# Decoder layer on one core: x loaded before the weights, split in two halves of its tokens, tile 0's low-weight products last

## The chip, the cores and the metric

One Trainium2 chip, one of its cores. The metric is the device time of one execution in microseconds (us); the kernel before takes 1079.82 us (median of 3 runs, 1078.2 to 1080.12). The engines are TensorE (PE, and PEld for its weight loads), VectorE (DVE), ScalarE (ACT), GpSimd (POOL) and SyncE (SP, which here issues nearly all DMAs).

## The reference

One layer of a decoder, 512 tokens, 1024 channels, all float32: RMSNorm, one input projection to three token mixers (RWKV-7, sparse attention, sliding-window attention) and to gates, merge, output projection, residual; then RMSNorm and a SwiGLU feed-forward with residual. What the change touches is only the first step:

```
y = x * rsqrt(mean(x*x) + eps) * g_pre_mix      # (512, 1024)
p = y @ w_in                                    # first columns: rwkv 0, 1, 2, ...
```

The kernel computes `(x * g_pre_mix)` transposed, multiplies it by the weights, and applies the row factor `rsqrt(...)` (`RINV`) when a result leaves PSUM.

## The kernel before

**Number format.** Products are as exact as float32 by splitting both sides in a high part (rounded to the engine's fp32r) and a low part (the rest). Each product of a chunk is three matmuls: high weight x high x (L1546), high weight x low x (L1547), low weight x high x (L1548). A weight tile `n` (1024 x 128) is loaded by SP to `WRAW` (four slots), its high part is written to `WHI` by ScalarE (L723; for tiles in `POOL_HI` by GpSimd, L609), its low part to `WLO` by GpSimd (L605). Semaphores `w_loaded`, `w_hi`, `w_lo` count them, in order of tiles. There are two slots of `WHI`/`WLO`, so the high part of tile n waits until tile n-2 is done.

**Tiles.** The jobs of `JOBS` run in order: tile 0 has 8 chunks `k` of 128 channels, each 3 matmuls of 128x128 weights by 512 tokens; its sum stands in PSUM bank 0, tile 1's in bank 1. `steps(c)` issues c chunks of the next tiles.

**The start.** SP issues x in four token tiles `x_in[t]` of 128 tokens x 1024 channels, the fourth after W0; then W1, `HOT`, `SNK`, `MASK`, W2, `SELT`, `WA`, W3; from W4 on each load waits for the low part of four tiles earlier. ScalarE issues the constants `CONP` (with the identity that transposes need) and the two parts of the parameter table `PRAW` on its own queue. TensorE transposes seven of eight channel blocks of x tiles 0, 1 and 2, then the table (its result goes to PSUM bank 7, and VectorE copies it to `PARC` in two pieces, `prow_ok`), then tile 3, then the eighth block of all four tiles, whose bank 7 the table had used. Bank k holds channel block k for all 512 tokens. ScalarE writes the high part of a block with its gain, `HHI[:, k]` (L739); VectorE writes the low part `HLO[:, k]` (L1106); chunk k of tile 0 waits for that (`xlo_ok`). Between them ScalarE squares and sums x tiles 0 and 2 and makes W0's high part; VectorE squares tiles 1 and 3 (L1096). From the sums come the root (L742), the reciprocal, four diagonal blocks (L1113, `diag_ok`) and, after four chunks of tile 1, one product (L1616) that spreads the factor over all partitions (`RINV`).

**The same pattern later.** The feed-forward's input is split in two halves of 256 tokens: `x1_transposes`, `h2_high` (L949) and `h2_low` (L1480), with the weights' products from L1961 on.

Of the kernel before, what the change touches and what calls it, by code (L numbers as in the profile page):

```python
# [24 lines left out]
F32 = mybir.dt.float32  # L25
# [8 lines left out]
KC = D // P  # L34
# [104 lines left out]
POOL_HI = [1] + list(range(NS0 + 4, MERGE0))  # L139
# [106 lines left out]
def build(nc, x, w_in, w_branch, w_out, w_gate, w_up, w_down, w2, a2, g2, ck1, ck2, cv1, cv2, sinks, rel_bias,  # L246
# [158 lines left out]

    def x1_block(h, k):
        return psum[(2, 3, 0, 1, 2, 3, 4, 6)[4 * h + k // 2]][:, 256 * (k % 2):256 * (k % 2) + 256]
# [124 lines left out]
    with block:  # L532
        @block.sync
        def _(sp):
# [3 lines left out]
            for t in range(3):  # L538
                x_tile(t)
            for n in range(FF0):  # L540
                if n == 1:
                    x_tile(3)
# [165 lines left out]
        def _(act):  # L708
# [7 lines left out]
            def hi_part(n):  # L716
# [4 lines left out]
                if n in (2, MERGE0):  # L721
                    act.wait_ge(w_hi, n)
# [9 lines left out]
            x_square(0)  # L732
            act.wait_ge(xsq_ok, 1)
            x_square(2)
            hi_part(0)
            act.wait_ge(prow_ok, 2)
            for k in range(KC):
                act.wait_ge(xT_done, k + 1)
                act.activation(HHI[:, k, :], psum[k][:, :], ACT.Identity, scale=par("g_pre_mix", k)).then_inc(xhigh_ok, 1)  # L739
# [282 lines left out]
        def _(dve):  # L1022
# [76 lines left out]
            x_square(1)  # L1099
            dve.wait_ge(prow_T, 1)  # L1100
            dve.tensor_copy(PARC[:, 0:NPAR1], R[5][:, 0:NPAR1]).then_inc(prow_ok, 1)
            dve.tensor_copy(PARC[:, NPAR1:NPAR1 + NPAR2], R[5][:, P:P + NPAR2]).then_inc(prow_ok, 1)
            dve.wait_ge(prow_ok, 2)
            for k in range(KC):
                dve.wait_ge(xhigh_ok, k + 1)
                dve.scalar_tensor_tensor(out=HLO[:, k, :], in0=psum[k][:, :], scalar=par("g_pre_mix", k),  # L1106
                                         in1=HHI[:, k, :].bitcast(F32), op0=ALU.mult, op1=ALU.subtract).then_inc(xlo_ok, 1)
# [422 lines left out]
        def _(pe):  # L1530
# [28 lines left out]
            def steps(count):  # L1559

                for _ in range(count):
# [11 lines left out]
                    if n == 0:  # L1573
                        pe.wait_ge(xlo_ok, k + 1)
# [6 lines left out]
                    if k == chunks - 1:  # L1581
                        last.then_inc(dense_done, 1)
                        dense["n"], dense["k"] = n + 1, 0

# [11 lines left out]
            def x_transpose(t, k):  # L1596
                return tr(psum[k][:, t * P:(t + 1) * P], XTOK0[:, t, k * P:(k + 1) * P])

            for t in range(3):
                pe.wait_ge(x_in[t], 16)  # L1600
                for k in range(KC - 1):
                    x_transpose(t, k)
# [3 lines left out]
            pe.wait_ge(x_in[3], 16)  # L1606
            for k in range(KC - 1):
                x_transpose(3, k).then_inc(xT_done, 1)
            pe.wait_ge(prow_ok, 2)
            for t in range(4):  # L1610
                last = x_transpose(t, KC - 1)
# [435 lines left out]
```

## Time and profile before

| | before |
|---|---|
| median of runs | 1079.82 us (1078.2 to 1080.12) |
| the profiled execution | 1081.36 us, span 1079.6 us |
| PE busy | 1045.2 us, 97% of the span |
| chain that ended last | PE 83%, DVE 9%, POOL 4% |
| mean granted clock of TensorE | 0.995 |

The profiled execution is one run, with its own time; its span is the stretch from the first to the last recorded instruction. In a timeline row the first number is the start from the span's start, the second the length; "x8" are eight instructions merged in one row; a bracket gives the idle time before and what ended it. A chain row tells which piece of work the end of the kernel hung on at that moment. Matmuls overlap: one takes 0.39 us from issue to end, while the next starts 0.23 us after it.

### The profile page before, as it was taken

To read this page: it belongs to the slowest core of one execution; us is meant where nothing else is said; L and a number is where in the kernel's file an instruction comes from. 1 tells how busy PE (TensorE), PEld (TensorE's weight loads), DVE (VectorE), ACT (ScalarE), POOL (GpSimd) and SP (SyncE) were. 2 spreads that over 40 slices of the span, in tenths; PEclk is the share of its full clock that TensorE was granted. 3 is DMA by queue.
4 is the path that set the end of the run, shared out by engine and by line. 5 is a ranking of instruction groups with operands and counts; after the bars stand their busy time and mean duration, and the time that the engine had idled before them with its cause. 6 is when DMAs were issued, how large, how long until landed. Compare 5 with 4: busy or idle time off the path is not lost.

```text
span 1079.6 us, 18610 instructions
## 1 busy us (share of the span) xinstructions
PE 1045.2 (97%) x7560; PEld 836.0 (77%) x7560; DVE 527.5 (49%) x882; ACT 355.8 (33%) x688; POOL 496.8 (46%) x409
## 2 busy tenths in 40 slices
PE   7989999999999999999989999999999999999997
PEld 6777778887787677766777777888888888888886
DVE  4775687466555545554552664144454545430004
ACT  4133332221322225444550445352222222221221
POOL 3365453113121446655777447534444444444462
PEclk9999999999999999999999999999999999999999
DMA  9334533002223453212112545603333333333322
GB/s 253 95 98 138 115 88 80 3 4 59 61 61 100 120 142 118 59 32 79 40 39 79 175 118 167 213 27 91 97 97 97 97 97 97 116 98 98 98 79 78
DMA packets 148784, 102.67 MB, mean 95 GB/s; under 512 B 20917, under 2 KB 131775, under 8 KB 148712
## 3 DMA queue, kind: packets, MB, share of 16 engines
q1 hardware_dynamic: 145516, 97.67, 31.9%
q10 hardware_dynamic: 3164, 3.97, 1.5%
q8 instruction: 53, 0.87, 0.4%
q14 instruction: 19, 0.16, 0.0%
q0 software_dynamic: 32, 0.00, 0.0%
HBM read 93.99 MB, written 7.63 MB: 94 GB/s over the span
## 4 chain that ended last, share of the span: by engine, by line
PE 83%; DVE 9%; POOL 4%; issue 2%; ACT 1%; DMA 1%; SPq 0%; ACTq 0%; DVEq 0%; POOLq 0%
PE ps L1546 17%; PE ps L1548 15%; PE ps L1547 15%; PE ps L1685 4%; PE ps L2001 4%; PE ps L2000 4%; PE ps L1999 4%; PE ps L1592 4%; PE ps L1845 3%; PE ps L1897 2%; DVE XF L1074 1%; PE ps L1921 1%; PE ps L1922 1%; PE ps L1923 1%; POOL WLO L605 1%
## 5 line engine op out<-in xcount | busy, mean ns | idle before, releaser
L605 POOL TENSOR_TENSOR WLO<-WRAW,WHI 128x1024 fp32r<-128x1024 f32 (+1 forms) x131 | 293.9, 2244 | 283.6 <-ACT WHI L723 158.0
L1546 PE MATMUL ps<-HHI,WHI 128*128 128x512 f32 x776 | 316.9, 408 | 5.1 <-POOL WLO L640 2.3
L1548 PE MATMUL ps<-HHI,WLO 128*128 128x512 f32 x776 | 304.3, 392 | 0.0
L1547 PE MATMUL ps<-HLO,WHI 128*128 128x512 f32 x776 | 304.1, 392 | 0.0
L1546 PEld LDWEIGHTS ps<-HHI,WHI 128*128 128x128 f32 x776 | 146.6, 189 | 57.7 <-issue 22.0
L1548 PEld LDWEIGHTS ps<-HHI,WLO 128*128 128x128 f32 x776 | 146.5, 189 | 32.0
L1547 PEld LDWEIGHTS ps<-HLO,WHI 128*128 128x128 f32 x776 | 146.8, 189 | 29.3 <-issue 1.9
L609 POOL CAST WHI<-WRAW 128x256 fp32r<-128x256 f32 (+1 forms) x78 | 49.2, 631 | 179.8 <-PE ps L1548 179.8
L723 ACT ACTIVATE WHI<-WRAW 128x1024 fp32r<-128x1024 f32 (+1 forms) x69 | 62.5, 907 | 159.4 <-PE ps L1548 82.0
L1504 DVE TENSOR_TENSOR FT<-FT 128x512 f32<-128x512 f32 x22 | 51.6, 2348 | 89.0 <-ACT FT L977 89.0
L870 ACT ACTIVATE EB<-EB,STAT 128x257 f32<-128x257 f32 (+5 forms) x96 | 50.4, 527 | 55.7 <-DVE STAT L1388 54.6
L971 ACT ACTIVATE WHI<-WRAW 128x1024 fp32r<-128x1024 f32 x40 | 42.3, 1057 | 71.7 <-PE ps L1548 71.7
L2001 PE MATMUL ps<-WLO,DHI 128*128 128x512 f32 x160 | 62.3, 389 | 0.0
L1999 PE MATMUL ps<-WHI,DHI 128*128 128x512 f32 x160 | 62.3, 389 | 0.0
L2000 PE MATMUL ps<-WHI,DLO 128*128 128x512 f32 x160 | 62.3, 389 | 0.0
L667 POOL TENSOR_SCALAR EB<-EB,STAT,GLT 128x128 f32<-128x128 f32 (+3 forms) x64 | 38.1, 608 | 33.2 <-DVE STAT L1404 33.0
L640 POOL TENSOR_TENSOR WLO<-WRAW,WHI 128x256 fp32r<-128x256 f32 x56 | 43.0, 768 | 4.6
L979 ACT ACTIVATE DHI<-FT 128x512 f32 (+1 forms) x22 | 13.9, 632 | 88.6 <-DVE FT L1509 88.6
L1388 DVE CUSTOM_DVE_ANT_0 EB<-ps,TB 128x128 f32<-128x128 f32 (+3 forms) x64 | 28.2, 488 | 25.3 <-PE ps L1845 25.3
L1546 PE MATMUL ps<-OHI,WHI 128*128 128x512 f32 x96 | 38.2, 398 | 2.0 <-POOL WLO L605 2.0
L1547 PE MATMUL ps<-OLO,WHI 128*128 128x512 f32 x96 | 37.4, 390 | 0.0
L1548 PE MATMUL ps<-OHI,WLO 128*128 128x512 f32 x96 | 37.4, 389 | 0.0
(311 smaller groups left out, 1608.1 us busy)
## 6 DMA issues: line engine op xcount, KB each, us to landing
WRAW<-in_w_in SPq DMA_DIRECT2D x47, 512.0 KB, 4.3
WRAW<-in_w_gate SPq DMA_DIRECT2D x22, 512.0 KB, 3.9
WRAW<-in_w_up SPq DMA_DIRECT2D x22, 512.0 KB, 3.9
WRAW<-in_w_down SPq DMA_DIRECT2D x22, 512.0 KB, 3.9
spilled<-SQ SPq DMA_DIRECT2D x21, 256.0 KB, 2.5
WRAW<-in_w_in SPq DMA_DIRECT2D x16, 256.0 KB, 3.6
WRAW<-in_w_branch SPq DMA_DIRECT2D x32, 128.0 KB, 2.9
WRAW<-in_w_out SPq DMA_DIRECT2D x8, 512.0 KB, 4.0
```

Source lines behind the costliest of these rows:

```text
L605: return pool.tensor_tensor(lo[:, 0:chunks, :], WRAW[:, n % NRAW, 0:chunks, :], hi[:, 0:chunks, :].bitcast(F32), ALU.subtract)
L609: return pool.tensor_copy(WHI[:, slot_of(n), k0:k1, :], WRAW[:, n % NRAW, k0:k1, :])
L723: act.activation(split_of(n)[0][:, 0:width_of(n), :], WRAW[:, n % NRAW, 0:width_of(n), :], ACT.Copy).then_inc(w_hi, 1)
L870: last = act.activation(EB[:, n % 3, g, cols], EB[:, n % 3, g, cols], ACT.Exp, scale=-1.0, bias=st[:, 0, u:u + 1], accum_out=st[:, 1, u:u ...
L1504: dve.tensor_tensor(FT[:, b + 1, :], FT[:, b + 1, :], FT[:, b, :], ALU.mult).then_inc(ff_x, 1)
L1546: pe.matmul(dst, WHI[:, s, k, :], hi, start=start, stop=False)
L1547: pe.matmul(dst, WHI[:, s, k, :], lo, start=False, stop=False)
L1548: return pe.matmul(dst, WLO[:, s, k, :], hi, start=False, stop=stop)
L1592: return pe.transpose(dst, src, ident[0:n, 0:n])
L1999: pe.matmul(dst, DHI[:, k, cols], whi, start=start, stop=False)
L2000: pe.matmul(dst, DLO[:, k, cols], whi, start=False, stop=False)
L2001: return pe.matmul(dst, DHI[:, k, cols], wlo, start=False, stop=stop)
```

## The change

- SP issues all four x tiles before W0.
- Banks 0 to 3 now hold all eight channel blocks of tokens 0 to 255, banks 4 to 7 those of tokens 256 to 511 (`x_block`). TensorE's order is x tile 0, the table, x tile 1, a wait for the copies to `PARC`, x tiles 2 and 3. `xT_done` counts pairs of blocks.
- ScalarE writes 16 high parts of 256 tokens instead of 8 of 512, behind the square of tile 0 and a wait for the copies; then comes the high part of W1 (it had W0's), then the square of tile 2. GpSimd makes W0's high part (it had W1's).
- VectorE copies the table before it squares tile 1 and writes 16 low parts of 256 tokens, each waiting for its pair of high parts (they share a bank).
- Tile 0's eight chunks issue their two products with the high weights first (wait `w_hi`), each after the low part of the second half; the eight products with the low weights come last, behind a wait for W0's low part.

```diff
--- before.py
+++ after.py
@@ -136,7 +136,7 @@
 NJ = len(JOBS)
 NRAW, NSPL = 4, 2
 
-POOL_HI = [1] + list(range(NS0 + 4, MERGE0))
+POOL_HI = [0] + list(range(NS0 + 4, MERGE0))
 
 SPILLED = list(range(SW0, GC0))
 NSTAGE = 2
@@ -402,6 +402,9 @@
 
     def down_bank(t, dh):
         return psum[4 + t if dh == 0 else t]
+
+    def x_block(h, k):
+        return psum[4 * h + k // 2][:, 256 * (k % 2):256 * (k % 2) + 256]
 
     def x1_block(h, k):
         return psum[(2, 3, 0, 1, 2, 3, 4, 6)[4 * h + k // 2]][:, 256 * (k % 2):256 * (k % 2) + 256]
@@ -535,11 +538,9 @@
             def x_tile(t):
                 sp.dma_start(XTOK0[:, t, :], x[t * P:(t + 1) * P, :]).then_inc(x_in[t], 16)
 
-            for t in range(3):
+            for t in range(4):
                 x_tile(t)
             for n in range(FF0):
-                if n == 1:
-                    x_tile(3)
                 if n == 2:
                     sp.dma_start(HOT[:, :], hot).then_inc(hot_in, 16)
                     sp.dma_start(SNK, bass.AP(sinks.tensor, 0, [[0, P], [1, NH]])).then_inc(hot_in, 16)
@@ -718,7 +719,7 @@
                 act.wait_ge(w_loaded[n % NRAW], loaded_value(n))
                 if slot_free(n):
                     act.wait_ge(dense_done, slot_free(n))
-                if n in (2, MERGE0):
+                if n in (1, MERGE0):
                     act.wait_ge(w_hi, n)
                 act.activation(split_of(n)[0][:, 0:width_of(n), :], WRAW[:, n % NRAW, 0:width_of(n), :],
                                ACT.Copy).then_inc(w_hi, 1)
@@ -730,13 +731,15 @@
                                accum_out=XSS[:, t:t + 1]).then_inc(xsq_ok, 1)
 
             x_square(0)
+            act.wait_ge(prow_ok, 2)
+            for h in range(2):
+                for k in range(KC):
+                    act.wait_ge(xT_done, 4 * h + k // 2 + 1)
+                    act.activation(HHI[:, k, 256 * h:256 * h + 256], x_block(h, k), ACT.Identity,
+                                   scale=par("g_pre_mix", k)).then_inc(xhigh_ok, 1)
+            hi_part(1)
             act.wait_ge(xsq_ok, 1)
             x_square(2)
-            hi_part(0)
-            act.wait_ge(prow_ok, 2)
-            for k in range(KC):
-                act.wait_ge(xT_done, k + 1)
-                act.activation(HHI[:, k, :], psum[k][:, :], ACT.Identity, scale=par("g_pre_mix", k)).then_inc(xhigh_ok, 1)
             act.wait_ge(xsq_ok, 2)
             act.wait_ge(xsum_ok, 2)
             act.activation(XRINV, XSS, ACT.Sqrt, scale=1.0 / D, bias=EPSC[:, 0:1]).then_inc(norm_std, 1)
@@ -1096,15 +1099,17 @@
                 dve.tensor_tensor_reduce(TMP[:, 0:2, :].rearrange("p a t -> p (a t)"), XTOK0[:, t, :], XTOK0[:, t, :],
                                          1.0, 0.0, ALU.mult, ALU.add, XSS[:, t:t + 1]).then_inc(xsum_ok, 1)
 
-            x_square(1)
             dve.wait_ge(prow_T, 1)
             dve.tensor_copy(PARC[:, 0:NPAR1], R[5][:, 0:NPAR1]).then_inc(prow_ok, 1)
             dve.tensor_copy(PARC[:, NPAR1:NPAR1 + NPAR2], R[5][:, P:P + NPAR2]).then_inc(prow_ok, 1)
+            x_square(1)
             dve.wait_ge(prow_ok, 2)
-            for k in range(KC):
-                dve.wait_ge(xhigh_ok, k + 1)
-                dve.scalar_tensor_tensor(out=HLO[:, k, :], in0=psum[k][:, :], scalar=par("g_pre_mix", k),
-                                         in1=HHI[:, k, :].bitcast(F32), op0=ALU.mult, op1=ALU.subtract).then_inc(xlo_ok, 1)
+            for h in range(2):
+                for k in range(KC):
+                    cols = slice(256 * h, 256 * h + 256)
+                    dve.wait_ge(xhigh_ok, 8 * h + 2 * (k // 2) + 2)
+                    dve.scalar_tensor_tensor(out=HLO[:, k, cols], in0=x_block(h, k), scalar=par("g_pre_mix", k),
+                                             in1=HHI[:, k, cols].bitcast(F32), op0=ALU.mult, op1=ALU.subtract).then_inc(xlo_ok, 1)
             dve.wait_ge(xsum_ok, 1)
             x_square(3)
             dve.wait_ge(norm_std, 1)
@@ -1570,8 +1575,6 @@
                             pe.wait_ge(xsplit_ok, i + 1)
                         if kind == "branch":
                             pe.wait_ge(olo_ok, 4 * (i % 3) + 4)
-                    if n == 0:
-                        pe.wait_ge(xlo_ok, k + 1)
                     hi, lo = rhs(n, k)
                     if kind == "cmp":
                         last = cmp_product(n, k, hi, lo, part == 0 and k == 0, part == 3 and k == 3)
@@ -1582,6 +1585,19 @@
                         last.then_inc(dense_done, 1)
                         dense["n"], dense["k"] = n + 1, 0
 
+            def first_tile():
+
+                pe.wait_ge(w_hi, 1)
+                for k in range(KC):
+                    pe.wait_ge(xlo_ok, KC + k + 1)
+                    pe.matmul(DB[0][:, :], WHI[:, 0, k, :], HHI[:, k, :], start=k == 0, stop=False)
+                    pe.matmul(DB[0][:, :], WHI[:, 0, k, :], HLO[:, k, :], start=False, stop=False)
+                pe.wait_ge(w_lo, 1)
+                for k in range(KC):
+                    last = pe.matmul(DB[0][:, :], WLO[:, 0, k, :], HHI[:, k, :], start=False, stop=k == KC - 1)
+                last.then_inc(dense_done, 1)
+                dense["n"] = 1
+
             def fill(point):
                 steps(FILL[point])
 
@@ -1593,24 +1609,23 @@
 
 
             pe.wait_ge(con_in, 16)
-            def x_transpose(t, k):
-                return tr(psum[k][:, t * P:(t + 1) * P], XTOK0[:, t, k * P:(k + 1) * P])
-
-            for t in range(3):
+            def x_transposes(t):
                 pe.wait_ge(x_in[t], 16)
-                for k in range(KC - 1):
-                    x_transpose(t, k)
+                for k in range(KC):
+                    at0 = P * (t % 2)
+                    last = tr(x_block(t // 2, k)[:, at0:at0 + P], XTOK0[:, t, k * P:(k + 1) * P])
+                    if t % 2 and k % 2:
+                        last.then_inc(xT_done, 1)
+
+            x_transposes(0)
             pe.wait_ge(par_in, 32)
             tr(R[5][:, 0:NPAR1], PRAW[0:NPAR1, 0, :], NPAR1)
             tr(R[5][:, P:P + NPAR2], PRAW[0:NPAR2, 1, :], NPAR2).then_inc(prow_T, 1)
-            pe.wait_ge(x_in[3], 16)
-            for k in range(KC - 1):
-                x_transpose(3, k).then_inc(xT_done, 1)
+            x_transposes(1)
             pe.wait_ge(prow_ok, 2)
-            for t in range(4):
-                last = x_transpose(t, KC - 1)
-            last.then_inc(xT_done, 1)
-            steps(8)
+            x_transposes(2)
+            x_transposes(3)
+            first_tile()
             steps(4)
             pe.wait_ge(diag_ok, 4)
             pe.matmul(R[4][:, :], ones, SSUM[:, :], start=True, stop=True).then_inc(norm_ss, 1)
```

## Rows read from the trace of the kernel before

**Rows 1.** Page, parts 1 and 4: busy time (share of the span), chain by engine

```profile
PE 1045.2 (97%) x7560; PEld 836.0 (77%) x7560; DVE 527.5 (49%) x882; ACT 355.8 (33%) x688; POOL 496.8 (46%) x409
...
PE 83%; DVE 9%; POOL 4%; issue 2%; ACT 1%; DMA 1%; SPq 0%; ACTq 0%; DVEq 0%; POOLq 0%
```

**Rows 2.** Chain of waits, 5 to 22 us: start, length, what

```profile
2.94 9.35 DMA XTOK<-in_x
...
12.34 2.61 PE ps L1592 x11
14.94 0.43 PE ps L1546
...
17.34 0.23 PE ps L1546
...
21.46 0.23 PE ps L1546
```

**Rows 3.** Timeline, 0 to 12 us, all engines

```profile
2.14 0.76 SPq L570 DMA_DIRECT2D WRAW<-in_w_in  x1
...
2.94 1.66 SPq L536 DMA_DIRECT2D XTOK<-in_x  x1
...
5.28 1.75 PE L1592 MATMUL ps<-CONP,XTOK 128*128 128x128 f32 x7 [5.28 <-DMA CONP<-in_con]
...
9.41 1.06 ACT L729 ACTIVATE SQ<-XTOK 128x1024 f32<-128x1024 f32 x1 [3.26 <-DMA XTOK<-in_x]
...
10.92 0.62 PE L1592 MATMUL ps<-CONP,PRAW 74*128 74x74 f32 x2
10.99 1.06 ACT L723 ACTIVATE WHI<-WRAW 128x1024 fp32r<-128x1024 f32 x1 [0.42 <-DMA WRAW<-in_w_in]
...
11.74 0.21 DVE L1102 COPY PARC<-ps 128x64 f32<-128x64 f32 x1
```

**Rows 4.** DMA issued at 2 to 3 us (landing), packets at 7:8, 8.5:8.8

```profile
WRAW<-in_w_in SPq DMA_DIRECT2D x1, 512.0 KB, 8.8
...
q10 hardware_dynamic: 24, 0.01, 3.7%
...
q10 hardware_dynamic: 4, 0.00, 1.5%
```

**Rows 5.** Timeline, 12 to 28 us, all engines

```profile
12.13 2.36 POOL L605 TENSOR_TENSOR WLO<-WRAW,WHI 128x1024 fp32r<-128x1024 f32 x1 [10.14 <-ACT WHI L723]
...
12.91 4.74 ACT L739 ACTIVATE HHI<-ps,PARC 128x512 fp32r<-128x512 f32 x8 [0.86 <-PE ps L1592]
...
13.70 5.36 DVE L1106 SCALAR_TENSOR_TENSOR HLO<-ps,PARC,HHI 128x512 fp32r<-128x512 f32 x8 [1.75 <-ACT HHI L739]
...
14.44 1.03 POOL L609 CAST WHI<-WRAW 128x1024 fp32r<-128x1024 f32 x1
...
18.98 1.22 DVE L1096 CUSTOM_DVE_ANT_0 TMP<-XTOK 128x1024 f32<-128x1024 f32 x1
...
20.85 0.88 DVE L1113 TENSOR_SCALAR SSUM<-CONP,MISC 128x128 f32<-128x128 f32 x4
...
24.02 1.02 PE L1616 MATMUL ps<-SSUM,CONP 128*128 128x512 f32 x2
```

**Rows 6.** Timeline, 700 to 727 us, feed-forward input, second half: ACT, DVE, PE

```profile
716.33 3.02 ACT L949 ACTIVATE HHI<-ps,PARC 128x256 fp32r<-128x256 f32 x8 [5.80 <-PE ps L1592]
...
717.20 3.23 DVE L1480 SCALAR_TENSOR_TENSOR HLO<-ps,PARC,HHI 128x256 fp32r<-128x256 f32 x8 [6.07 <-ACT HHI L949]
...
717.74 0.39 PE L1961 MATMUL ps<-HHI,XWHI 128*128 128x256 f32 x1 [1.45 <-DVE HLO L1480]
```

**Rows 7.** Timelines of POOL and DVE, 0 to 90 us

```profile
36.53 2.40 POOL L605 TENSOR_TENSOR WLO<-WRAW,WHI 128x1024 fp32r<-128x1024 f32 x1 [5.11 <-ACT WHI L723]
...
36.78 2.69 DVE L1130 SCALAR_TENSOR_TENSOR RW<-PSH,PARC,RW 128x512 f32<-128x512 f32 x1
...
75.83 0.75 DVE L1130 SCALAR_TENSOR_TENSOR RW<-PSH,PARC,RW 128x512 f32<-128x512 f32 x1
```

## Prediction

> **What bounds the kernel now.** I read the page's busy times and chain first. TensorE is busy 97% of the span and holds 83% of the chain that ended last [rows 1]; almost everything between about 17 us and the end is a queue of 512-column products at 0.23 us each. A change in the first 20 us is therefore worth exactly what it moves the moment at which that queue starts, and nothing more, as long as nothing behind it becomes late.
>
> The chain of waits for the first 22 us says what sets that moment [rows 2]: the fourth token tile of x is issued at 2.94 and lands 9.35 us later, at 12.29; eleven transposes follow until 14.94; then tile 0's 24 products. The first five of them stand 0.43 us apart and the later ones 0.23. These are the two levels of the engine's clock, 1.2 and 2.4 GHz (the ratio is 1.87), although the granted clock prints as full; the engine had been busy without a break since 12.34 when the spacing fell at 17.1 to 17.3. Tile 1's first product starts at 21.46. The reference point of the whole sum is this 21.46: "tile 0 done".
>
> Then the timeline of each engine, to see who could have started earlier [rows 3]. The seven transposes of a token tile take 1.75 us (0.22 us each, low clock). The transposes of the parameter table start at 10.92, and VectorE's two copies, which everything that scales by `g_pre_mix` waits for, end at 11.95. Before, the table's transposes stand behind three x tiles, so one cannot see when the table really landed, only that it was by 10.9.
>
> **What replaces the wait.** The wait for x tile 3 goes. SP issues it in the slot in which W0 was issued (2.14 instead of 2.94 [rows 3]), and the transfers land roughly in order of issue: x tile 2 by 9.4, W0 at 10.98 (2.14 + 8.8 [rows 4]), x tile 3 at 12.29. Swapped, x tile 3 lands at about 11.0 and W0 at about 12.3. What is late next is the parameter table. In the new order its transposes stand in front of those of x tile 1, so that its landing holds TensorE, both copies on VectorE, and through them ScalarE's first high part. The table comes on ScalarE's own queue, q10. That queue still moves 24 packets between 7 and 8 us and 4 between 8.5 and 8.8 [rows 4]. So the table lands after 8.8 and before 10.92. I take 9.5, since x tile 2, whose packets shared the engines with it until then, lands at 9.37. TensorE thus goes idle after x tile 0, from about 7.1 to 9.5: the earlier x tile buys nothing until then.
>
> The Trainium skill, "DMA: Bandwidth & Descriptors", section "Why a DMA increments its semaphore by 16 and not by 1", says that a transfer is dealt over the largest number of engines up to 16 that divides its rows, which makes two for 74 rows. It would explain why 37 KB trickle for so long; the packet counts show the trickle, no row shows the two engines.
>
> **The sum, from T = 9.7, the first product of the table's transposes** (9.5 plus the 0.2 us of a weight load). Offsets are those of before: copies done at T + 1.03 (11.95 - 10.92) = 10.73; TensorE free at T + 0.62 = 10.3.
>
> - x tile 1: 8 transposes x 0.22 = 1.8, until 12.1; tile 2 until 13.8, tile 3 until 15.6 at the low clock. Tile 3 has landed long before.
> - ScalarE, half 0: its first high part came 0.57 us after the transpose that it needed (12.34 to 12.91 [rows 2, 5]); now it needs the pair, so 10.52 + 0.57 = 11.1. A 128x256 high part is not in the first 20 us, but the same form stands at the FFN's input: 8 in 3.02 us [rows 6], 0.365 apart. Half 0 runs 11.1 to 14.1.
> - VectorE: square of x tile 1 now stands behind the copies: 10.75 + 1.22 [rows 5] = 12.0. Then 8 low parts of half 0 at 3.23 us per eight [rows 6], 0.394 apart: 12.05 to 15.2. High parts are ahead of them.
> - ScalarE, half 1: first pair of tile 3 starts at 14.0, + 0.57 = 14.6 (14.3 if the clock is up by then); high parts until 17.4. VectorE half 1 starts when both are ready, 15.2 to 15.45.
> - TensorE's first product of tile 0: in the FFN's pair of rows the first product comes 0.54 us after the first low part starts (717.20 to 717.74 [rows 6]): 15.85. Later low parts come every 0.394 us and two products take 0.454, so TensorE is never held again; the last low part is due at 18.6, its product at 19.0.
> - 24 products x 0.227 = 5.45, taken at the high level, since TensorE then has been at work from 9.5, with a pause of 0.2 at most (before, it had worked from 12.34 when the spacing fell at 17.3): tile 0 done at 21.3, against 21.46. Gain 0.16, call it 0.2 us.
>
> The first product starts 0.9 us later than before (15.85 against 14.94), and the 1.07 us that the slow products cost there (21.46 - 14.94 = 6.52, less 5.45) comes back. Bounds: the landing anywhere from 8.8 to 10.7 shifts everything by -0.7 to +1.2.
>
> **Costs that I put at nothing, and their cover.** W0's high part on GpSimd: W0 at 12.3 plus one cast of 1.03 [rows 5] is 13.4, cover 2.4 us before 15.85. Its low part (2.36 [rows 5]) ends at 15.8; it is needed after 16 products, at 19.5. The products of the low weights placed last cost the same 8 x 0.227, wherever they stand. W1's high part on ScalarE now stands behind 16 high parts: 1.06 [rows 3], 17.4 to 18.5, its low part until 20.9; TensorE wants it at 21.3: cover 0.4 us, the thinnest. Norm of x: square of tile 3 starts at 18.5 and the chain from there to the last diagonal took 2.75 us before (18.98 to 21.73 [rows 5]), so 21.3; needed after 12 products of tile 1, at 24.0. ScalarE's x square of tile 2 (1.06 [rows 3]) falls in the gap between W1's high part and the root. W2's high part waits behind the root, 0.3 to 0.8 later than before, and tile 2 is wanted only after 24 more products. SP waits for W0's low part before it issues W4, 1.3 us later (15.8 against 14.5), and for W1's before W5 (20.9 against some 17.8); four earlier loads still fill the queue, and tile 4 is wanted not before 21.46 + 3 x 5.45 = 37.8.
>
> One cover is at risk. A VectorE operation with two SBUF inputs does not run beside a GpSimd one: the `L1130` operation takes 0.75 alone but 2.69 when it starts inside a low part of 36.53 to 38.93, and ends 0.5 after it [rows 7]. The new square of tile 3 starts at 18.5, just as W1's low part does. If GpSimd is first, the square ends at about 21.9 and the diagonals at 23.4, still before 24.0. If VectorE is first, W1's low part ends up to 1.2 later, at 22.1, and TensorE stands 0.8 us. The Trainium skill, "GPSIMD Engine Reference", section "Specifications", says the same: the SBUF interfaces are shared, with contention for VectorE instructions with two SBUF inputs. The low parts of half 0 and 1 read one input from PSUM, and before they ran beside two GpSimd operations at 0.67 us each.
>
> **Own time.** The profiled execution took 1081.36 us with a span of 1079.6; the median of the runs is 1079.82, 1.5 lower, with runs from 1078.2 to 1080.12. The gain of 0.2 is applied to the median: 1079.6 us.
>
> **Rivals.**
>
> A, the forecast: the table's landing takes the place of x tile 3's. 1079.6. Chance 0.59.
>
> B, the table is there by 7.1, q10's late packets being something else. TensorE never idles, T = 7.3, tile 0 done 2.4 earlier in all clocked alike, less a few slow products: 1077.6. For it: nothing shows the landing itself. Against: the packets until 8.8, and q10 carries only the table after the constants. Chance 0.13.
>
> C, the clock rises at the same point as before, 17.1, not earlier: three or four of tile 0's products at 0.43, +0.6 to 0.8 on A: 1080.3. Against: the unbroken work begins 2.6 us sooner. Chance 0.10.
>
> D, the port: VectorE's square gets in front of W1's low part, TensorE stands 0.8 us at tile 1: 1080.4. Chance 0.07.
>
> E, slower: x tile 3's 4 KB packets now stand where W0's 512 B ones stood, and q10's packets share the DMA engines with them. If the table is pushed back until x tile 3 is through, it lands at 12.3, where x tile 3 landed before; T = 12.5, tile 0 done at 24.1, + 2.7: 1082.5. It decides from a landing of 11.8 on. For it: the table was slow beside 4 KB packets before. Against: its last packets go out by 8.8, while x tile 2 is still on its way, so few turns are left to lose. Chance 0.11. The Trainium skill, "DMA: Bandwidth & Descriptors", section "Queues, rings and completion order", says that a DMA engine takes turns between queues packet by packet, which is the mechanism of E; by that rule each turn lost costs one 4 KB packet.
>
> **How the numbers follow.** No change can be told from one of less than 0.2%, 2.2 us. A, C and D lie inside; B is at that edge (0.10 of its 0.13 beyond it, as a table landing before 7 would bring nothing more and the runs scatter by 1 us), and A's low tail adds 0.05: faster 0.15. E gives 0.08 beyond, the upper tails of A, C and D 0.04: slower 0.12. Same 0.73. Range for 8 in 10: from B's time, 1077.6, to the landing at its late bound on top of A with the scatter of the runs, 1081.6. The likeliest case's own range is 1078.7 to 1080.8.
>
> **What would show it.** TensorE idle from about 7 to 9.5 us with the release by the table's DMA; the copies to `PARC` ending near 10.7; ScalarE's half 0 from 11.1 and VectorE's half 1 from 15.3; first product of tile 0 near 15.9 at the high clock; tile 1's first product near 21.3, no wait on `WLO`; the norm's product near 24.0. The prediction is wrong if TensorE does not idle before the table (B), if it idles beyond 11 (E), if the low parts do not follow each other at 0.39, or if a stage after 25 us does not simply move along with tile 0.

## The result, and the profile after

The changed kernel takes 1081.53 us (median of 16, 1079.87 to 1083.32) against 1079.95 (16, 1078.07 to 1080.76) for the kernel before on the same chip: a ratio of 1.0018, interval 1.001 to 1.0026. A second comparison gave 1081.75 against 1080.22, 1.0026 (1.0017 to 1.0035). It is slower by about 1.6 us. The prediction was 1079.6, 0.2 us faster; the measured time lies just inside its range for 8 in 10 (1077.6 to 1081.6) and above the range of its likeliest case (1078.7 to 1080.8).

The page of the changed kernel, its busy times, beside [rows 1]. The profiled execution took 1080.04 us with a span of 1078.2, and so looks shorter than the one of before; why is told at the end.

```profile
PE 1042.4 (97%) x7560; PEld 834.4 (77%) x7560; DVE 530.6 (49%) x890; ACT 356.1 (33%) x696; POOL 497.6 (46%) x409
```

The counts fit the edit: eight operations more on VectorE and on ScalarE, none on TensorE. The chain of waits of the same trace, 0 to 22 us (start, length, what), beside [rows 2]:

```profile
1.79 7.24 DMA PRAW<-in_par
...
9.07 4.73 PE ps L1608 x20
...
16.85 0.96 ACT WHI L724
...
17.87 3.43 POOL WLO L606
21.35 0.50 PE ps L1551
```

Where the chain of before began with x tile 3, this one begins with the parameter table. It ends in something that the chain of before did not have: tile 1 waits for the low part of W1, which takes 3.43 us instead of 2.4. The timeline of the same trace (a bracket is the idle time before, and its releaser):

```profile
9.07 0.68 PE L1608 MATMUL ps<-CONP,PRAW 74*128 74x74 f32 x2 [1.80 <-DMA PRAW<-in_par]
...
15.32 0.47 PE L1593 MATMUL ps<-HHI,WHI 128*128 128x512 f32 x1 [0.36 <-DVE HLO L1111]
...
21.35 0.50 PE L1551 MATMUL ps<-HHI,WHI 128*128 128x512 f32 x1 [0.34 <-POOL WLO L606]
```

In this execution T, the first product of the table's transposes, is 9.07, and tile 1 starts at 21.35, as before, where the timeline has tile 0's and tile 1's first products at

```profile
14.60 0.77 PE L1546 MATMUL ps<-HHI,WHI 128*128 128x512 f32 x1
...
21.30 0.39 PE L1546 MATMUL ps<-HHI,WHI 128*128 128x512 f32 x1
```

Such a start explains no 1.6 us. So the first question was whether this trace is typical.

### The profile page after: what moved, and what is told of

Same layout as the page of the kernel before. It is cut to its first block, busy times and chain, and to the rows that moved or that the text cites. A ratio compares the mean times of both kernels' runs of the same rounds, so it can differ in the third digit from the quotient of the medians.

```text
span 1078.2 us, 18628 instructions
## 1 busy us (share of the span) xinstructions
PE 1042.4 (97%) x7560; PEld 834.4 (77%) x7560; DVE 530.6 (49%) x890; ACT 356.1 (33%) x696; POOL 497.6 (46%) x409
## 4 chain that ended last, share of the span: by engine, by line
PE 82%; DVE 9%; POOL 4%; issue 2%; ACT 2%; DMA 1%; ACTq 0%; DVEq 0%; POOLq 0%
PE ps L1551 16%; PE ps L1553 15%; PE ps L1552 15%; PE ps L1700 4%; PE ps L1608 4%; PE ps L2016 4%; PE ps L2014 4%; PE ps L2015 4%; PE ps L1860 3%; PE ps L1912 2%; POOL WLO L606 1%; DVE XF L1077 1%; PE ps L1936 1%; PE ps L1938 1%; PE ps L1937 1%
## 5 line engine op out<-in xcount | busy, mean ns | idle before, releaser
L1551 PE MATMUL ps<-HHI,WHI 128*128 128x512 f32 x768 | 312.3, 407 | 5.4 <-POOL WLO L641 2.3
L1553 PE MATMUL ps<-HHI,WLO 128*128 128x512 f32 x768 | 300.0, 391 | 0.0
L1552 PE MATMUL ps<-HLO,WHI 128*128 128x512 f32 x768 | 299.5, 390 | 0.0
L1551 PEld LDWEIGHTS ps<-HHI,WHI 128*128 128x128 f32 x768 | 144.2, 188 | 57.9 <-issue 22.1
L1553 PEld LDWEIGHTS ps<-HHI,WLO 128*128 128x128 f32 x768 | 144.2, 188 | 31.3
L1552 PEld LDWEIGHTS ps<-HLO,WHI 128*128 128x128 f32 x768 | 144.5, 188 | 28.6 <-issue 1.9
```

The source lines that it names most:

```text
L1551: pe.matmul(dst, WHI[:, s, k, :], hi, start=start, stop=False)
L1552: pe.matmul(dst, WHI[:, s, k, :], lo, start=False, stop=False)
L1553: return pe.matmul(dst, WLO[:, s, k, :], hi, start=False, stop=stop)
```

## The experiments

The theories: **D**, VectorE's square stretches W1's low part (the expectations call it the stall theory); **C**, the clock; **S**, something after 25 us does not move along with tile 0; and **L**, formed only after the second trace, the table lands later than in the first trace in most executions, because x tile 3's packets stand beside it (the prediction's E in part). "Tile 1" below is the start of its first product: in the two traces of before 21.30 and 21.64, mean 21.47.

**The changed kernel again, timed and traced** (no edit).

> The changed kernel once more, as it is, to have a second trace and the spread on this chip. Clock theory: the two kernels do the same work in the same time at the same clock (the traces at hand are 0.2 us apart at 47 us and 0.3 at the end once one low-clock stretch of before is taken out), and the 1.6 us of the medians come from TensorE being at its low clock more often or longer; then times come in groups about 1.7 us apart and tile 0 ends at 20.6 in some traces and up to 1.7 later in others. Stall theory: the whole difference is the 0.76 us that TensorE stands before tile 1 and what it sets off; then tile 0 ends at 20.6 and tile 1 starts at 21.3 in each trace, and the time is 1080 to 1082.

Measured: 1081.75 us (11 runs) against 1080.22, 1.0026 (1.0017 to 1.0035). Timeline:

```profile
10.39 0.68 PE L1608 MATMUL ps<-CONP,PRAW 74*128 74x74 f32 x2 [3.11 <-DMA PRAW<-in_par]
...
12.73 6.50 DVE L1111 SCALAR_TENSOR_TENSOR HLO<-ps,PARC,HHI 128x256 fp32r<-128x256 f32 x16
...
16.64 0.47 PE L1593 MATMUL ps<-HHI,WHI 128*128 128x512 f32 x1 [0.79 <-DVE HLO L1111]
...
19.15 1.21 DVE L1099 CUSTOM_DVE_ANT_0 TMP<-XTOK 128x1024 f32<-128x1024 f32 x1
19.19 3.43 POOL L606 TENSOR_TENSOR WLO<-WRAW,WHI 128x1024 fp32r<-128x1024 f32 x1 [3.16 <-ACT WHI L724]
...
22.67 0.50 PE L1551 MATMUL ps<-HHI,WHI 128*128 128x512 f32 x1 [0.31 <-POOL WLO L606]
```

T is 10.39, TensorE idles 3.11 us for the table, and everything stands 1.32 us later than in the first trace, offset by offset: first product at T + 6.25 in both, tile 1 at T + 12.28 in both. Neither of the two theories of the expectation has a late table. What came true of it is that the times fall into groups (1081.6 to 1081.8 and 1082.7 to 1083.5). Of the traces that follow, all with this order of loads have T at 10.4 or later and the first one is the exception. How rare it is among executions is not shown: in the first comparison seven of 16 runs lie at 1079.9 to 1080.7, near its own 1080.04, in this one none of 11.

**Each kernel once more**, a third trace of the change and a second of before.

> The changed kernel, for one more trace. If the table lands late as a rule: its transposes at 10.3 to 10.8. If the first trace (9.07) is the rule: 9.0 to 9.3.

> The kernel before, for a second trace. x tile 3 lands at 12.2 to 12.6, tile 1 starts at 21.2 to 21.6, and q10's last packets go out by 9.0; a landing of x tile 3 that varies by over 0.5 us would say that the start of before is no firmer than that of the change.

First the change (1083.14 us), then before (1079.95):

```profile
10.46 0.68 PE L1608 MATMUL ps<-CONP,PRAW 74*128 74x74 f32 x2 [3.27 <-DMA PRAW<-in_par]
...
22.74 0.50 PE L1551 MATMUL ps<-HHI,WHI 128*128 128x512 f32 x1 [0.31 <-POOL WLO L606]
```

```profile
12.25 1.42 PE L1592 MATMUL ps<-CONP,XTOK 128*128 128x128 f32 x11 [1.00 <-DMA XTOK<-in_x]
...
21.64 0.39 PE L1546 MATMUL ps<-HHI,WHI 128*128 128x512 f32 x1
```

Mean of the change's two later traces 22.70, of before 21.47: + 1.23 of the 1.6 us, all of it ahead of 23 us. Tile 0's first products are not always fast before the change either: in the second trace of before eight of them come 0.4 us apart, five in the first, which is why tile 1 starts 0.34 later there.

**The change with x tile 3 behind W0 again**: only SP's order is undone.

```
-            for t in range(4):
+            for t in range(3):
                 x_tile(t)
             for n in range(FF0):
+                if n == 1:
+                    x_tile(3)
```

> The changed kernel with x tile 3 issued behind W0 again, as in the kernel before. Turn theory (the table's packets on q10 take turns with what SP's queue has at the front of each DMA engine, and behind 4 KB rows of x tile 3 a turn is dearer than behind 512 B runs of W0): q10's last packets go out by 9.0 instead of 9.5 to 10.3, the table's transposes start at 9.2 to 9.8 instead of 10.4 to 10.7, x tile 3 lands at 12.3, just in time for its transposes; median 0.7 to 1.2 us below the changed kernel's. Rival (the table is late whatever stands in SP's queue): start at 10.4 to 10.7 in the trace, same median as the changed kernel, 1081.7.

Measured: 1081.34 us (11) against 1080.20, 1.0014 (1.0005 to 1.0023).

```profile
9.62 0.68 PE L1610 MATMUL ps<-CONP,PRAW 74*128 74x74 f32 x2 [2.19 <-DMA PRAW<-in_par]
...
21.89 0.50 PE L1553 MATMUL ps<-HHI,WHI 128*128 128x512 f32 x1 [0.34 <-POOL WLO L608]
```

The trace is as the turn theory expected: T is 0.8 us earlier, and so is tile 1. The median is not: it is 0.2 to 0.4 us below the changed kernel's two medians instead of 0.7 to 1.2.

**Before with x tile 3 ahead of W0**, the same edit alone, the other way:

```
-            for t in range(3):
+            for t in range(4):
                 x_tile(t)
             for n in range(FF0):
-                if n == 1:
-                    x_tile(3)
```

> The kernel before with one edit, x tile 3 issued ahead of W0. If the late table is what the early x tile costs: x tile 3 lands at 10.1 to 10.6, but the table's transposes, which stand before those of tile 3, now start at 10.4 to 10.9 and let them follow at 11.5; tile 1's first product 0.5 to 0.8 us earlier than the 21.3 of before, median 1079.4 to 1079.9. If the early x tile alone made the kernel slower: above 1081.

Measured: 1081.45 us (11) against 1080.20, 1.0014 (1.0003 to 1.0024); an execution of 3606.67 us is left out.

```profile
10.84 0.49 PE L1590 MATMUL ps<-CONP,PRAW 74*128 74x74 f32 x2 [0.21 <-DMA PRAW<-in_par]
11.26 1.42 PE L1590 MATMUL ps<-CONP,XTOK 128*128 128x128 f32 x11
...
15.96 0.50 PE L1544 MATMUL ps<-HHI,WHI 128*128 128x512 f32 x1 [3.28 <-POOL WLO L603]
...
23.14 0.39 PE L1544 MATMUL ps<-HHI,WHI 128*128 128x512 f32 x1
```

L stands. With x tile 3 ahead of W0, T was 10.39, 10.46, 10.56, 10.70, 10.70 and 10.84 in six traces of five kernels (the first trace's 9.07 is the seventh); with W0 ahead 9.62, with nothing else changed. The last packet of q10, ScalarE's queue, tells the same and can be seen where the table's landing is hidden too: it starts at 8.6, 8.7 and 8.9 in the three traces with W0 ahead (two of before, and the change with W0 ahead), at 9.7 to 10.1 in the six with x tile 3 ahead, and at 8.5 in the first trace, whose cause stays open.

The swap alone makes the old kernel slower too, against what its expectation put first (0.5 to 0.8 us gained at tile 1, a median of 1079.4 to 1079.9). It is another wait that does it: x tile 3's transposes start 1.1 us sooner (11.26 against 12.34 [rows 2]), but TensorE then stands 3.28 us for W0's low part, eight of tile 0's products come 0.4 us apart, and tile 1 starts at 23.14. That wait is the one that placing the low products last hides: in the change W0's low part ends at 16.0 and is wanted at 20.4.

The packets say how the swap delays the table. DMA of a stretch by queue (packets, MB, share of 16 engines), 8.0 to 8.5 us: before, then the change again.

```profile
q1 hardware_dynamic: 259, 0.15, 110.4%
q10 hardware_dynamic: 8, 0.00, 2.7%
```

```profile
q1 hardware_dynamic: 54, 0.19, 96.1%
q10 hardware_dynamic: 7, 0.00, 2.4%
```

And the change again from 9.0 to 9.5 us, where before, its repetition and the kernel with W0 ahead have no q10 packet left:

```profile
q1 hardware_dynamic: 287, 0.16, 112.2%
q10 hardware_dynamic: 6, 0.00, 2.0%
```

SP's queue moves 259 packets in half a microsecond when they are W0's 512 B, and 54 when they are x's 4 KB. An estimate from the shares in these rows (16 engines, 0.5 us): one took 0.03 us when small, 0.14 when large. Against the small ones q10 gets its last packets out by 9.0, against the large ones 8 are left (6 here, 2 until 10.0). The Trainium skill, "DMA: Bandwidth & Descriptors", section "Queues, rings and completion order", says that an engine alternates between queues packet by packet; the runs agree with it in kind, since q10 is slower beside the larger packets. How many of the profile's packets go in one turn no row shows.

The landing of x tile 3 itself, issued at 2.14 in the change again (the last number is the time from issue to landing):

```profile
XTOK<-in_x SPq DMA_DIRECT2D x1, 512.0 KB, 8.5
```

So x tile 3 lands at 10.6, 0.2 us behind T: in this order the table does come in with the end of x tile 3. In the first trace x tile 3 takes 7.9 us, until 10.1, and the table is there 1.0 us before it.

**The table's first part as 64 + 10 rows**, in the change and in before (the same edit in `consts`, with the wait on 48):

```
-            act.dma_start(PRAW[0:NPAR1, 0, :], par1).then_inc(par_in, 16)
+            act.dma_start(PRAW[0:64, 0, :], par1[0:64, :]).then_inc(par_in, 16)
+            act.dma_start(PRAW[64:NPAR1, 0, :], par1[64:NPAR1, :]).then_inc(par_in, 16)
```

> The changed kernel with the first part of the parameter table loaded in two DMAs, of 64 and of 10 rows, instead of one of 74. Theory of the forecast (the table's landing sets the start): it lands by 7 us instead of 9.0, the copies end by 8.3, half 0 starts at 8.6, and tile 0's first product at 13.5 to 13.9, 1.5 to 1.8 us earlier; the time falls by as much. Rival (the rows are not what makes it late, the queue is): it lands at 9 as before and nothing changes.

> The kernel before with the table's first part in DMAs of 64 and of 10 rows. There the table's landing is hidden behind three x tiles. If the 74 rows also hold back what shares their DMA engines, x tile 3 lands at 11.3 to 11.5 instead of 12.3 and the time falls by 0.8 us; if they cost only themselves, nothing changes, median within 0.3 us of the kernel before.

Measured: the change 1079.38 us (11) against 1080.22, 0.9999 (0.999 to 1.0007); before 1078.54 (12) against 1080.20, 0.9991 (0.9983 to 1.0). Timelines, the change first:

```profile
8.51 0.68 PE L1609 MATMUL ps<-CONP,PRAW 74*128 74x74 f32 x2 [1.25 <-DMA PRAW<-in_par]
...
20.79 0.50 PE L1552 MATMUL ps<-HHI,WHI 128*128 128x512 f32 x1 [0.30 <-POOL WLO L606]
```

```profile
11.26 2.37 PE L1593 MATMUL ps<-CONP,XTOK 128*128 128x128 f32 x11 [1.68 <-DMA XTOK<-in_x]
...
19.72 0.39 PE L1547 MATMUL ps<-HHI,WHI 128*128 128x512 f32 x1
```

T comes 1.9 us earlier in the change (8.5, where 7 was expected), tile 1 as well, and the median falls by 2.4. So the table's landing is what the changed kernel waits for. But the same edit helps the kernel before too, by 1.7 us, twice the 0.8 that its expectation named for this case: x tile 3 lands at 11.2 instead of 12.3. The 74-row load had slowed the x tiles as well. The Trainium skill, "DMA: Bandwidth & Descriptors", section "Why a DMA increments its semaphore by 16 and not by 1", has a rule by which 74 rows go to two engines; both kernels agree with it, in that 64 + 10 rows move faster and clear the way for others, though no row shows which engines carried them. With the split in both, the change stays behind: tile 1 at 20.79 against 19.72, and 0.8 us in the medians, about half of the original loss; the two ratios' intervals overlap, so the 0.8 rests on the traces more than on the times.

**The table's first part on SP's queue, ahead of x**, in the change, without and with the square of x tile 3 on ScalarE:

```
+            sp.dma_start(PRAW[0:64, 0, :], par1[0:64, :]).then_inc(par_in, 16)
+            sp.dma_start(PRAW[64:NPAR1, 0, :], par1[64:NPAR1, :]).then_inc(par_in, 16)
             for t in range(4):
```

> The changed kernel with the table's first part in front of x on SP's queue, in DMAs of 64 and of 10 rows, and nothing else: c1_sp_table with the square of x tile 3 back on VectorE. Theory: copies at 8.5, tile 0's first product at 13.7 as there; W1's low part meets the square again and takes 3.4 us, 15.9 to 19.3, so that tile 1 starts 0.3 us later at most; what ScalarE's square seemed to cost at 290 us (0.3) does not occur; the median is within 0.5 us of c1_sp_table's. Rival (the port collision matters): 0.7 to 1.5 us slower than c1_sp_table.

> The changed kernel with the table's first part in front of x on SP's queue, in DMAs of 64 and of 10 rows, and the square of x tile 3 on ScalarE. Theory: table there before x tile 0 is transposed, its transposes at 7.3 to 7.6, tile 0's first product at 13.5 to 14.0 against 15.3 to 16.6, no stop before tile 1, tile 1's first product at 19.2 to 19.8; 1.5 to 2 us below the kernel before, 1078.2 to 1078.8. Rival (an early start meets W0, the clock or the weights instead): tile 1's first product at 20.5 or later and 1079.4 or more.

Measured: 1079.78 us (11), 0.9995 (0.9986 to 1.0003), T 7.79, tile 1 19.41; with the square on ScalarE 1079.20 (12, two of them at 1612 and 1717 us; 1078.5 without these), 0.9991 (0.998 to 1.0001), T 7.62, tile 1 19.24. This is rival B made real: T at about 7.7 gives a start 2.1 us ahead of before's, and medians lower by only 0.4 and 1.7. The lead is not lost in the trace of the first: it took 1077.99 us, 2.0 less than the second trace of before. What differs between its runs (four at 1077.9 to 1078.5, seven at 1079.6 to 1080.5) is taken up under "From 1.2 to 1.6 us". Its expectation failed on both counts: W1's low part was not stretched, since GpSimd started ahead of VectorE, and the median is over 0.5 us above the second kernel's (1.3 without that one's two long executions), on another chip. The rows of the first:

```profile
16.10 2.41 POOL L608 TENSOR_TENSOR WLO<-WRAW,WHI 128x1024 fp32r<-128x1024 f32 x1 [0.29 <-ACT WHI L725]
...
16.36 3.22 DVE L1100 CUSTOM_DVE_ANT_0 TMP<-XTOK 128x1024 f32<-128x1024 f32 x1
...
19.41 0.39 PE L1552 MATMUL ps<-HHI,WHI 128*128 128x512 f32 x1
```

Here the square pays (3.22 instead of 1.21 us) and TensorE does not stand. The expectation for the second held: tile 1 at 19.24 without a stop before it (19.2 to 19.8 expected), and 1078.5 without the two long executions (1078.2 to 1078.8).

**The square of x tile 3 on ScalarE alone**:

```
             act.wait_ge(xsq_ok, 2)
-            act.wait_ge(xsum_ok, 2)
+            x_square(3)
+            act.wait_ge(xsq_ok, 3)
+            act.wait_ge(xsum_ok, 1)
...
-            dve.wait_ge(xsum_ok, 1)
-            x_square(3)
```

> The changed kernel with the square of x tile 3 on ScalarE (behind that of tile 2) instead of VectorE, so that nothing of VectorE's with two SBUF inputs meets W1's low part on GpSimd. Stall theory: the low part takes 2.4 us instead of 3.4, is done at 20.3, TensorE goes from tile 0 to tile 1 without a stop at 20.6, and the time falls by 0.7 to 1.6 us. Clock theory: by 0.7 at most in executions with an early clock, by nothing in those with a late one; the spread stays.

Measured: 1082.65 us (8), 1.0025 (1.0015 to 1.0036).

```profile
19.50 2.40 POOL L606 TENSOR_TENSOR WLO<-WRAW,WHI 128x1024 fp32r<-128x1024 f32 x1 [3.16 <-ACT WHI L724]
...
22.48 0.39 PE L1551 MATMUL ps<-HHI,WHI 128*128 128x512 f32 x1
```

T is 10.70 here. W1's low part is back at 2.40, and tile 1 starts at T + 11.78 without a wait, 0.50 sooner than T + 12.28. So D is shown as a mechanism and sized, 0.5 us, at this place. In the medians it does not show (1082.65 against 1081.75, intervals overlapping), though 0.7 to 1.6 us less was expected. A part is given back: near 290 us TensorE waits 1.0 us for VectorE's `ST` in this trace and in the other one with the square on ScalarE, 0.7 in all others. Its eight runs lie at 1081.5 to 1081.8 and 1082.6 to 1083.5, as those of the change do.

**Ten transposes of nothing after x tile 0**, so that TensorE works while it waits for the table:

```
             x_transposes(0)
+            for _ in range(10):
+                tr(psum[7][:, 256:384], ident)
```

> The changed kernel with ten further transposes of the identity (2.2 us at 0.22) behind those of x tile 0, into a part of bank 7 that is written again later, so that TensorE does not idle from 7 to 9 us. Clock theory: the clock rises earlier and in every execution before tile 0, the upper groups of times go, median 1.0 to 1.7 us below the changed kernel's. Stall theory: no change within 0.5 us.

Measured: 1081.93 us (12), 1.0018 (1.0009 to 1.0027). Timeline, then the windows (length, busy time and count of each engine, granted clock, DMA share, GB/s):

```profile
10.98 2.84 PE L1608 MATMUL ps<-CONP,XTOK 128*128 128x128 f32 x24
...
16.34 0.47 PE L1593 MATMUL ps<-HHI,WHI 128*128 128x512 f32 x1 [2.52 <-DVE HLO L1111]
...
23.50 0.39 PE L1551 MATMUL ps<-HHI,WHI 128*128 128x512 f32 x1
```

```profile
16.70:20.10 3.40, 3.40 (x10) 2.62 (x9) 3.40 (x7) 2.78 (x6) 1.58 (x1) 0.50 1.12 168
```

The transposes are done by 13.8, two us earlier than the 15.9 of the change again, for their work at the high clock (0.12 us each instead of 0.20). It buys nothing: the first product waits 2.52 us for VectorE's low part, and during tile 0's products the granted clock is 0.50, a stretch in which the change has 1.00. The products then stand 0.43 us apart, and tile 1 starts at 23.50, 0.8 later than in the change. The median is the same as the change's (1081.75): the gain of 1.0 to 1.7 us that the clock theory expected did not come. Against C as the cause of the slowdown speaks that the change's own products stand 0.23 apart from the first on, as forecast.

**The table's transposes behind those of x tile 1**, in the change:

```
             x_transposes(0)
+            x_transposes(1)
             pe.wait_ge(par_in, 32)
...
-            x_transposes(1)
             pe.wait_ge(prow_ok, 2)
```

> The changed kernel with the table's transposes behind those of x tile 1 instead of in front. Theory (behind the table it is ScalarE's and VectorE's 32 parts that set the start, not TensorE's transposes): TensorE works from 7.3 to 9.1 instead of idling, the table's transposes start when it lands (10.4), and tile 0's first product comes at most 0.3 us earlier; median as the changed kernel's within 0.5 us. Rival (TensorE's order sets it): 1.3 to 1.8 us earlier and faster by as much.

Measured: 1080.98 us (12) against 1080.16, 1.0019 (1.0009 to 1.0028).

```profile
10.70 0.68 PE L1608 MATMUL ps<-CONP,PRAW 74*128 74x74 f32 x2 [1.32 <-DMA PRAW<-in_par]
...
16.68 0.76 PE L1593 MATMUL ps<-HHI,WHI 128*128 128x512 f32 x1 [1.08 <-DVE HLO L1111]
...
23.77 0.39 PE L1551 MATMUL ps<-HHI,WHI 128*128 128x512 f32 x1
```

TensorE idles 1.32 us instead of 3.11, and the first product hardly moves (16.68 against 16.64, behind a T that is 0.31 later: T + 5.98 instead of T + 6.25). So TensorE's transposes are not what stands between the table and the first product. It is VectorE's row of low parts. But tile 0's first products stand 0.43 us apart in this trace, until 19.8, and tile 1 starts 1.1 us later than in the change, while the median is 0.6 to 0.8 us lower than the change's (within 0.5 was expected). The start of tile 1 alone does not give the time; the next part says what else counts.

## Why the prediction was wrong, by its steps

**The step that failed is "I take 9.5" for the table's landing**, with the reason given against rival E, "few turns are left to lose". T is 10.39 and 10.46 in the two later traces of the change and 10.6 to 10.8 in all others with x tile 3 ahead of W0 and the table as it was; forecast was 9.7. I had read q10's last packets, at 8.8 in the trace of before [rows 4], as a property of q10. They went with W0's small packets beside them: between 7.5 and 9.0 us the queue had 18 packets left to send, and they were sent more slowly when the other queue's packets grew from 512 B to 4 KB. Eight came out after 9.0. E's mechanism came, at a smaller price. E let the table land with x tile 3, and T and x tile 3's landing are 0.2 us apart in both later traces; but it priced this at 12.3, x tile 3's landing in the old order, where the prediction itself had put it at 11.0 in the new one, and it was 10.6. So the cost was 0.7 to 0.8 us against the forecast, and 0.8 against the 9.62 with W0 ahead. It lay inside the bound that I gave the landing, + 1.2, and I had put too little of the chance there.

**Rival D came on top, not in its place.** "If VectorE is first, W1's low part ends up to 1.2 later ... TensorE stands 0.8 us." VectorE was first by 0.03 to 0.04 us in all three traces of the change, the low part took 3.42 to 3.43 instead of 2.4, and tile 1 stood some 0.5 us: 24 products at 0.227 after 16.64 would end at 22.1, and tile 1 starts at 22.67. I had it at 0.07, as an accident of timing. But VectorE was first by the same 0.03 to 0.04 us in the traces of the two other kernels that keep this order of work, with W0 ahead and with 64 + 10 rows. So it seems a property of this order of instructions (in three of the kernels above that shift this moment, GpSimd was first); that it is so in every execution is not shown.

**The size of both**: the landing + 0.7, the first product + 0.1 later behind T, and D + 0.6, on the forecast 21.3, are 22.7; measured 22.67 and 22.74. Against 21.47 of before that is + 1.2. I had also compared my 21.3, a start by the timeline, with 21.46, a start by the chain, where the earlier product's end is cut off; by the timeline before starts at 21.30, so that even the promised 0.16 us was none. That the first trace of the change has tile 1 at 21.35, as forecast, is luck: T came 0.6 us sooner than forecast there, and D took 0.6.

**What held.** From T on, the working was right. First product at T + 6.25 (forecast T + 6.15); low parts 0.41 us apart (0.394), high parts 0.38 (0.365); tile 0's products at the high clock from the first in all three traces of the change (C fell); the eight low-weight products last, ready in time (19.04 in the first trace, W0's low part done 15.4); the norm's product at 24.2 with tile 1 at 21.35 (forecast 24.0 with 21.3). B, the table by 7.1, occurred in no trace of the change.

**Break-even.** Tile 1 starts at T + 12.28, in before at 21.47: the change loses from T = 9.2 on, or from 9.7 without D. The first trace, 9.07, lay just on the good side. And once the table is early in both, the change still is behind by 1.07 us at tile 1 (20.79 against 19.72). About 0.5 of this is D, which this trace has too (W1's low part took 3.43). The rest is argued, from the work ahead of the first product: VectorE must make nine low parts of 256 tokens (the eight of half 0 and one of half 1) before it can start, 16.64 - 12.73 = 3.91 us after it began. Before, one low part of 512 tokens was enough, and VectorE's first one began 0.9 us before the product (13.70 [rows 5], 14.60). Two halves cost 6.50 us of VectorE in all where one pass cost 5.36 [rows 5]; an early half 0 was to hide this, and even with the table at 8.5 it did not. x tile 3 arriving sooner was worth nothing, since VectorE was at half 0 until about 16.

**From 1.2 to 1.6 us.** The times of both kernels come in groups some 1.7 to 2 us apart (before 1078.0 to 1078.6 and 1079.7 to 1081.4; the change 1079.9 to 1080.7 and 1081.5 to 1083.3). What sets them apart in the traces is the granted clock. After a gap of 2.2 us in which TensorE waits for VectorE's scaling of the output, until 67.0 in before, it is low for a while in one execution and not in another. The windows of 66 to 73 us, of before, of its second trace, of the change again and of the change's first trace (the number before the DMA share is the granted clock):

```profile
66.00:73.00 7.00, 6.00 (x19) 4.80 (x20) 5.56 (x6) 1.85 (x2) 5.17 (x2) 0.76 0.44 125
```

```profile
66.00:73.00 7.00, 5.68 (x26) 4.68 (x26) 5.88 (x6) 2.14 (x3) 5.20 (x2) 1.00 0.44 133
```

```profile
66.00:73.00 7.00, 4.82 (x16) 3.68 (x15) 6.76 (x7) 2.93 (x3) 5.17 (x2) 0.77 0.49 145
```

```profile
66.00:73.00 7.00, 5.80 (x27) 4.80 (x28) 5.80 (x7) 2.01 (x3) 5.19 (x2) 1.00 0.45 131
```

Such a stretch costs 0.24 x 7 us = 1.7 us. A second one lies near 115 us in all traces but one. The number n of such stretches between tile 1 and 122 us can be read off the granted clock of the window 60 to 122 us: it is 0.94 with two, 0.97 with one and 1.00 with none. With it the traces come out alike:

| trace | tile 1 | n | span | span - tile 1 - 1.7 n |
|---|---|---|---|---|
| before; again | 21.30; 21.64 | 2; 1 | 1079.6; 1078.1 | 1054.9; 1054.8 |
| before, x tile 3 first | 23.14 | 1 | 1079.7 | 1054.9 |
| before, 64 + 10 rows | 19.72 | 2 | 1078.1 | 1055.0 |
| change; again; third | 21.35; 22.67; 22.74 | 1; 2; 2 | 1078.2; 1081.3; 1081.3 | 1055.2 each |
| change, W0 first | 21.89 | 1 | 1078.8 | 1055.2 |
| change, 64 + 10 rows | 20.79 | 1 | 1077.4 | 1054.9 |
| change, table on SP; with the square on ScalarE | 19.41; 19.24 | 1; 2 | 1076.1; 1078.0 | 1055.0; 1055.4 |
| change, square on ScalarE | 22.48 | 1 | 1080.0 | 1055.8 |
| change, ten transposes | 23.50 | 1 | 1080.3 | 1055.1 |
| change, table late | 23.77 | 0 | 1079.1 | 1055.3 |

This settles three things. The start of tile 1 carries through to the end, to within some 0.3 us in most kernels; what hides it in the times is n, which varies from execution to execution and from kernel to kernel. Traces of two kernels must be compared at the same n: before's second trace and the change's first, with n = 1 both, differ by 0.1 us in their times, since the table was early in the latter; before's first and the change again, with n = 2, by 1.7. And the last column is 0.3 us larger in the three traces of the change than in the two of before. That is theory S. At about 630 us, in the merge, TensorE waits once more for a low part of weights. Its waits from 600 to 700 us, of before and of the change again (total, times, longest):

```profile
PE ps L1546 <- POOL WLO L605: 2.0, 6, 0.3
```

```profile
PE ps L1551 <- POOL WLO L606: 2.3, 7, 0.3
```

So the loss is 1.23 us ahead of tile 1 and 0.3 at 630 us, 1.6 in all, at equal n. The wait at 630 is not tied to the order of loads alone: it is absent in the change with 64 + 10 rows and present in before with 64 + 10 rows; what decides it is open. Open too is what makes n what it is, and whether an early table landing, as in the first trace, and the lower group of the change's times go together: only the profiled executions show n and T. Not tried: the low-weight products last alone, in the order of before.

## What to carry to other kernels

When loads are reordered, ask of every load on another queue what size the packets beside it will have: the small load of 74 rows came in 0.8 us later beside 4 KB packets than beside those of 512 B, and its landing in the old order is no forecast for the new one. Splitting such a load so that its rows divide well (64 + 10 here) was worth more than the whole reordering: the kernel before with this one edit took 1078.54 us, 0.9991 (0.9983 to 1.0), at the edge of what the runs can tell, and nothing measured here was faster beyond the scatter. And before a pass is cut in two halves, count how many pieces then stand ahead of the first result that the bounding engine wants: nine small ones against a single large one. When single traces of two kernels are compared, take out the low-clock stretches first: one of them is worth more than this whole change.

## What the hardware showed that I had not expected

- A load of 74 rows and 37 KB held back loads of half a megabyte: with it as 64 + 10 rows x tile 3 landed at 11.2 instead of 12.3 us.
- What VectorE's square and GpSimd's low part cost together depends on who is first by 0.04 us, and the second one pays for nearly the whole of the first: VectorE's square 1.21 and GpSimd's low part 3.43 one way, 3.22 (3.12 and 3.15 in two other kernels) and 2.41 the other way. ScalarE's square beside a low part took 1.06.
- More work on TensorE ahead of a wait can make what follows slower: ten idle transposes gave a high clock to 24 transposes that nobody waited for, and half the clock (0.50 from 16.7 to 20.1) to the products. In the time it did not show (1081.93 against 1081.75).
- One kernel's executions differ by a low-clock stretch at 68 us or near 115 us that comes in one and not in the next, 1.7 us each; with these and the start of tile 1 taken out, 13 of 14 traces agree within 0.6 us where their spans differ by up to 5.2.
